# Attention jobs of the two layers: heads paired across the key groups, values of four jobs as one product

## The reference

```python
q = partial_rope(rmsnorm_2(q, q_norm[l]), cos, sin)          # 16 heads
k = partial_rope(rmsnorm_2(k, k_norm[l]), cos, sin)          # 2 heads
a_out = sliding_window_attention(q, k, v, sinks[l])
c_out = conformer_conv(u, ug, conv_w[l], conv_b[l], conv_ln_g[l],
                       conv_ln_b[l], w_conv_out[l])
merged = jax.nn.sigmoid(ga) * a_out + jax.nn.sigmoid(gb) * c_out
x = x + jnp.einsum('btd,de->bte', merged, w_out[l])
```

## Time and profile before

| | |
|---|---|
| median of 3 runs | 2248.43 us (2248.36 to 2249.26) |
| span of the profiled execution | 2246.4 us |
| TensorE busy | 2224.9 us, 99% |
| VectorE busy | 1245.1 us, 55% |
| ScalarE busy | 885.6 us, 39% |
| GpSimd busy | 280.7 us, 12% |
| granted TensorE clock | 0.999 of full |
| stage of the job loop | 1033 to 1155 us and, the second time, 1725 to 1847 us |

### The profile page before, as it was taken

The page is one execution under the profiler, slowest core; times in us unless marked ns, Lnnn a source line. Parts: engine busy times, 40 slices in busy tenths (PEclk is TensorE's granted clock), DMA queues, the critical chain, the costliest instruction groups (busy, mean ns, idle before and its releaser), DMA issues.

```text
span 2246.4 us, 29245 instructions
## 1 busy us (share of the span) xinstructions
PE 2224.9 (99%) x11388; PEld 1821.7 (81%) x11388; DVE 1245.1 (55%) x1836; ACT 885.6 (39%) x1363; POOL 280.7 (12%) x273
## 2 busy tenths in 40 slices
PE   9999999999999999999999999999999999999999
PEld 7877888898888888886778888888887668888887
DVE  6467656445444225999664444333889664544422
ACT  5545454354333225234744333222323753433321
POOL 3000032011000001014331000001003442000000
PEclk9999999999999999999999999999999999999999
DMA  6221033122222231321122222222221112322222
GB/s 223 100 76 57 20 121 126 55 72 99 103 102 93 94 113 69 113 75 57 56 77 81 107 93 93 100 106 105 104 84 57 39 66 85 113 102 104 94 101 86
DMA packets 30484, 203.19 MB, mean 90 GB/s; under 512 B 3504, under 2 KB 4144, under 8 KB 6704
## 3 DMA queue, kind: packets, MB, share of 16 engines
q1 hardware_dynamic: 29088, 197.34, 24.4%
q10 hardware_dynamic: 1296, 4.46, 0.5%
HBM read 199.69 MB, written 2.10 MB: 90 GB/s over the span
## 4 chain that ended last, share of the span: by engine, by line
PE 93%; DVE 3%; POOL 1%; ACT 1%; issue 1%; DMA 0%; ACTq 0%; DVEq 0%; POOLq 0%
PE bank L415 26%; PE bank L417 26%; PE bank L416 26%; PE bank L2110 1%; PE bank L1002 1%; PE bank L2120 1%; PE bank L2133 1%; PE bank L973 1%; PE bank L2028 1%; POOL acc L324 1%; PE bank L990 1%; PE bank L2010 1%; PE bank L1593 1%; PE bank L1570 1%; PE bank L515 1%
## 5 line engine op out<-in xcount | busy, mean ns | idle before, releaser
L415 PE MATMUL bank<-x_hi,w_hi 128*128 128x512 f32 (+1 forms) x2032 | 789.9, 389 | 5.9 <-DVE x_lo L1766 2.3
L417 PE MATMUL bank<-x_hi,w_lo 128*128 128x512 f32 (+1 forms) x2032 | 775.0, 381 | 0.0
L416 PE MATMUL bank<-x_lo,w_hi 128*128 128x512 f32 (+1 forms) x2032 | 774.1, 381 | 0.0
L301 DVE TENSOR_TENSOR w_lo<-w_raw,w_hi 128x2048 fp32r<-128x2048 f32 x167 | 386.2, 2313 | 412.3 <-ACT w_hi L297 412.3
L297 ACT ACTIVATE w_hi<-w_raw 128x2048 fp32r<-128x2048 f32 x167 | 319.7, 1916 | 585.8 <-PE bank L417 583.9
L415 PEld LDWEIGHTS bank<-x_hi,w_hi 128*128 128x128 f32 x2032 | 382.1, 188 | 83.6 <-issue 6.8
L417 PEld LDWEIGHTS bank<-x_hi,w_lo 128*128 128x128 f32 x2032 | 381.9, 188 | 74.9
L416 PEld LDWEIGHTS bank<-x_lo,w_hi 128*128 128x128 f32 x2032 | 382.4, 188 | 72.7 <-issue 2.9
L415 PE MATMUL bank<-f_hi,w_hi 128*128 128x512 f32 (+1 forms) x572 | 213.3, 373 | 0.0
L416 PE MATMUL bank<-f_lo,w_hi 128*128 128x512 f32 (+1 forms) x572 | 213.2, 373 | 0.0
L417 PE MATMUL bank<-f_hi,w_lo 128*128 128x512 f32 (+1 forms) x572 | 213.2, 373 | 0.0
(11 more groups left out here) (355 smaller groups left out, 2637.2 us busy)
## 6 DMA issues: line engine op xcount, KB each, us to landing
w_raw<-w_d SPq DMA_DIRECT2D x184, 1024.0 KB, 4.8
out_d<-h SPq DMA_DIRECT2D x8, 256.0 KB, 6.6
h<-x_d ACTq DMA_DIRECT2D x3, 512.0 KB, 9.2
tab<-rope_d ACTq DMA_DIRECT2D x2, 640.0 KB, 3.9
memT<-mem_d ACTq DMA_DIRECT2D x1, 1024.0 KB, 4.8
w_raw<-w_d SPq DMA_DIRECT2D x2, 256.0 KB, 4.1
h<-x_d ACTq DMA_DIRECT2D x2, 256.0 KB, 5.8
w_raw<-w_d SPq DMA_DIRECT2D x1, 512.0 KB, 6.6
```

The source lines that it names most:

```text
L301: dve.tensor_tensor(w_lo[:, u.slot, :], w_raw[:, u.slot, :], w_hi[:, u.slot, :], ALU.subtract).then_inc(lo_ready, 1)
L415: pe.matmul(dst, wh[:, k, cols], hi[:, kx_, at:at + width], start=start, stop=False)
L416: pe.matmul(dst, wh[:, k, cols], lo[:, kx_, at:at + width], start=False, stop=False)
L417: return pe.matmul(dst, wl[:, k, cols], hi[:, kx_, at:at + width], start=False, stop=stop)
```

## The change

- Query heads are stored so that tile t holds head t on the lower and head 8 + t on the upper half of the partitions. Both halves then find their keys in place: lkx and its two ScalarE copies a layer go. The host orders the columns of the query, attention gate and convolution gate weights, of the convolution's output weights, the rows of the output weights and the sinks to match.
- The value product takes a group of four jobs (two in block 0): lprobT holds four jobs side by side, one matmul moves up to 512 columns. There are ten groups, in steps 7, 11, 15, 19, 23, 27, 29, 31, 33 and 35, and each stands between the scores and the transposes of its step. The gating is one VectorE instruction a group.
- FILL_AT deals the same 75 chunks out otherwise: fewer in the steps with values, more in others.
- VectorE merges tiles 3, 5 and 7, GpSimd 0, 1, 2, 4 and 6. MERGE_HI_AT goes from 29 to 31, MERGE_LO_AT from 30 to 32, and OUT_AT from one tile in each of steps 32 to 35 to tile 0 in step 32, tile 1 in 34, tiles 2 and 3 in 35.

```diff
@@ scratch @@
-        lkx = place("lkx", [P, T], F32, a)
-        lprobT = place("lprobT", [P, 2, 4, P], F32, b)
+        lprobT = place("lprobT", [P, 2, 2, 4, P], F32, b)
@@ groups and schedule @@
+        GROUPS = [range(j, j + 4) for j in range(0, 24, 4)] + [range(j, j + 2) for j in range(24, LJ, 2)]
+        NG = len(GROUPS)
+        GROUP_OF = [n for n, js in enumerate(GROUPS) for _ in js]
+        VALUES_AT = {js[-1] + LAG_V: n for n, js in enumerate(GROUPS)}
-        FILL_AT = {1: 6, 2: 2, 3: 1, 5: 4, 6: 4, 7: 2, 9: 3, 10: 2, 12: 3, 14: 6, 15: 5, 16: 3, 17: 4, 18: 4, 19: 2,
-                   20: 3, 21: 2, 22: 1, 23: 2, 24: 2, 25: 2, 26: 1, 27: 2, 28: 2, 29: 3, 30: 3, 31: 1}
+        FILL_AT = {1: 6, 2: 3, 4: 1, 5: 4, 6: 4, 7: 1, 8: 3, 9: 3, 10: 2, 12: 3, 13: 2, 14: 3, 15: 1, 16: 4, 17: 3, 18: 3,
+                   19: 1, 20: 4, 21: 3, 22: 3, 23: 1, 24: 3, 25: 3, 26: 2, 27: 1, 28: 3, 29: 1, 30: 3, 31: 1}
-        MERGE_HI_AT, MERGE_LO_AT = 29, 30
-        OUT_AT = {32: (0,), 33: (1,), 34: (2,), 35: (3,)}
+        MERGE_HI_AT, MERGE_LO_AT = 31, 32
+        MERGED_BY_DVE, MERGED_BY_POOL = (3, 5, 7), (0, 1, 2, 4, 6)
+        OUT_AT = {32: (0,), 34: (1,), 35: (2, 3)}
@@ TensorE @@
-                    keys = key_rows(lq[:, 8, :], lkx[:, :], e, g)[:, k0:(i + 1) * P]
+                    keys = lq[HD * e:HD * e + HD, 8, k0:(i + 1) * P]
-            def values(j):
+            def values(n):
+                js, cols = GROUPS[n], group_cols(n)
-                pe.wait_ge(A["turned_copied"], L * LJ + j + 1)
+                pe.wait_ge(A["turned_copied"], L * LJ + js[-1] + 1)
...
-                        mm = pe.matmul(bank[HD * e:HD * e + HD, 6, 0:P], lv[:, i - 1 + c, g * HD:(g + 1) * HD],
-                                       lprobT[:, j % 2, 2 * e + c, :], start=(c == first), stop=(c == 1))
+                        mm = pe.matmul(bank[HD * e:HD * e + HD, 6, cols.start * P:cols.stop * P], lv[:, i - 1 + c, e * HD:(e + 1) * HD],
+                                       lprobT[:, e, c, cols, :].rearrange("p m t -> p (m t)"), start=(c == first), stop=(c == 1))
@@ order of a step @@
+                if t in VALUES_AT:
+                    values(VALUES_AT[t])
                 if 0 <= t - LAG_T < LJ:
                     turn(t - LAG_T)
                 fill_chunks(FILL_AT.get(t, 0))
...
-                if 0 <= t - LAG_V < LJ:
-                    values(t - LAG_V)
@@ ScalarE @@
-                if n == ROPE_UNITS[0] + 2:
-                    act.wait_ge(q_rope, L * 9 + 1)
-                    act.activation(lkx[0:HD, :], lq[HD:P, 8, :], ACT.Copy).then_inc(l_kx, 1)
-                    act.activation(lkx[HD:P, :], lq[0:HD, 8, :], ACT.Copy).then_inc(l_kx, 1)
-                if j >= 2:
-                    act.wait_ge(A["pv"], L * LJ + j - 1)
+                if j >= 4:
+                    act.wait_ge(A["pv"], L * NG + GROUP_OF[j - 4] + 1)
@@ VectorE @@
-                if 0 <= t - LAG_V < LJ:
-                    gated(t - LAG_V)
-                if t == STEPS - 1:
-                    dve.wait_ge(A["gated"], L * LJ + LJ)
-                    dve.wait_ge(mg_sum, L * 8 + 7)
-                    dve.wait_ge(co_ready, L * 8 + 8)
-                    dve.tensor_tensor(sgb[:, 7, :], sgb[:, 7, :], sga[:, 7, :], ALU.add).then_inc(mg_sum, 1)
+                if t in VALUES_AT:
+                    gated(VALUES_AT[t])
+                if t in (LJ - 1, LJ + 1, LJ + 3):
+                    k = MERGED_BY_DVE[(t - LJ + 1) // 2]
+                    dve.wait_ge(A["gated"], L * NG + GROUP_OF[24 + k] + 1)
+                    dve.wait_ge(co_ready, L * 8 + k + 1)
+                    dve.tensor_tensor(sgb[:, k, :], sgb[:, k, :], sga[:, k, :], ALU.add).then_inc(mg_sum_dve, 1)
@@ GpSimd @@
-                    if j > 28:
-                        merged(L, j - 29)
-                for k in range(LJ - 28, DT - 1):
+                    if j in (LJ - 2, LJ - 1):
+                        merged(L, j - LJ + 2)
+                for k in MERGED_BY_POOL[2:]:
                     merged(L, k)
```

More of the change, by code:

```diff
@@ L2098, in scores @@
             def scores(j):
[L2099 removed]
+                i, tile = block_of(j), j % 8
                 if j == 0:
[L2101 removed]
                     pe.wait_ge(l_g, L * 16 + 10)
@@ L2419, in softmax, with gated @@
                     dve.reciprocal(asm(o, 12), asm(o, 4)).then_inc(A["rec"], 1)
[L2421 to L2425 removed]
+            def gated(n):
+                js, cols = GROUPS[n], group_cols(n)
+                i, tile = block_of(js[0]), js[0] % 8
+                dst = sga[:, tile:tile + len(js), i * P:(i + 1) * P]
+                dve.wait_ge(A["pv"], L * NG + n + 1)
+                if n == 0:
                     dve.wait_ge(l_g, L * 16 + 8)
[L2427 removed]
+                pv = bank[:, 6, cols.start * P:cols.stop * P].rearrange("p (m t) -> p m t", t=P)
+                dve.scalar_tensor_tensor(out=dst, in0=dst, scalar=1.0, in1=pv, op0=ALU.add, op1=ALU.mult).then_inc(A["gated"], 1)
             def conv_gated(k):
@@ L2699 @@
     stream += ffn_units(g["w_gate_up"], g["w_down"])
+    paired = np.concatenate([np.r_[HD * t:HD * t + HD, HD * (8 + t):HD * (8 + t) + HD] for t in range(8)])
+    sink_order = np.arange(16).reshape(2, 8).T.reshape(-1)
     for l in range(LAYERS):
```

47 lines of the change are left out of this document (26 added, 21 removed).

## The result

The changed kernel is slower: 2258.94 us (2257.43 to 2260.06) against 2248.68 (2248.36 to 2249.26) for the kernel before, ratio 1.0044 with a 95% interval of 1.0032 to 1.0056, so 10.3 us. The forecast was 2252.2 us, with a range up to 2256.5: the direction held, the size did not.

What follows compares the result with a forecast made beforehand. TensorE, busy 99% of the span, was taken as the bound. Per layer, 0.75 us gained before the last fill less 2.6 lost at the end, doubled, made a 3.7 us loss on 2248.43: 2252.2 us, range 2242.5 to 2256.5.

Steps and rivals of the forecast that it cites:

- Part 1: Value products in TensorE's queue: four jobs as one product take 1.87 us instead of 2.36, saving 3.0 us a layer.
- F: End of the last fill product in a layer's attention stage, 1141.94 us in the kernel before.
- Part 2: Dropping the swapped keys and their two ScalarE copies a layer: 0, bound a gain of 0.7 us a layer.
- Part 3: New order before the last block: new TensorE waits cost 0.3, 0.15 and 1.8 us a layer.
- the column sums: At step 7 TensorE comes earlier and waits longer for GpSimd: cost 0.3 us a layer.
- step 12: Its transposes wait for ScalarE's copy because step 11 has no fill: cost 0.15 us a layer.
- ScalarE's chain: Steps 14 to 17: step 17's transposes wait for ScalarE's chain, cost 1.8 us a layer, bounds 0 and 2.1.
- The net before F: Balance before the last fill: 3.0 - 0.3 - 0.15 - 1.8, about +0.75 us gained a layer.
- Rivals 1 and 4: Waits stay small, 2244.5 us, chance 0.20; or TensorE's savings and waits cancel, 2248.4 us, chance 0.20.
- rival 3: The 512-column value pairs do not overlap: 10 us a layer more, about 2270 us; chance 0.02.
- part 4: End of the stage, last fill to output product k=4: loss of 0.8 to 4.4 us a layer, 2.6 taken.
- rival 2: The tail's far end: VectorE loses the port at k=0, k=1 and k=3, 2255.7 us; chance 0.18.

Runs made afterwards that it cites:

- e2: Kernel before with paired heads, no swapped keys and groups of four in the first 24 jobs, old fill and old end: 2245.85 us against 2248.11.
- e1: Kernel before with only paired heads and no swapped keys, groups of one, old fill, merges and output products: 2248.44 us against 2248.11.
- e4: Changed kernel with ten spare TensorE products before output product k=0 and six before k=1: 2253.55 us against 2248.11 for the kernel before.
- e8: Changed kernel with tile 7 alone merged by VectorE, tiles 0 to 6 by GpSimd: 2252.87 us against 2249.13 for the kernel before.
- e9: Changed kernel, GpSimd's first merges a step earlier, halves from steps 30 and 31, o_lo before gating, VectorE merging only tile 7: 2247.59 us against 2248.96 before.
- e12: e9 with two fill chunks moved from step 17 to step 16: 2245.64 us against 2248.96 for the kernel before.
- e10: e2 with the new fill up to step 12, then the old less a chunk in steps 14, 19 and 23: 2244.70 us against 2248.96 before.
- e11: e10 with high and low halves of the output tiles one step later, from steps 30 and 31: 2261.16 us against 2248.96 for the kernel before.

## Why the prediction was wrong

**Right.** The bound, and that the waits of TensorE decide. Part 1: 1.87 a group was predicted and 1.86 measured; 3.0 us a layer predicted and 2.6 measured, in e2 and in the changed kernel alike (there 0.6 net plus 2.0 of new waits before F: 0.81 + 0.17 + 0.57 + 0.15 + 1.49 = 3.2 against 1.2); the rest is short waits that the list leaves out. Part 2 at nothing: e1. Part 3: the column sums 0.3 predicted and 0.57 - 0.26 = 0.31 measured; step 12 0.15 predicted and 0.85 - 0.63 = 0.22 measured (1074.34 to 1075.19); ScalarE's chain 1.8 predicted and 0.15 + 1.49 = 1.64 measured (TensorE's side of that sum is 3.3 + 3.8 + 4.0 + 0.6 = 11.7, not 11.6, so it gives 1.7). The net before F was predicted at +0.75 a layer and is +0.6. Rivals 1 and 4 fell with the waits at the end, and rival 3 with the 1.86.

**The step that failed is part 4,** the end of the stage, taken as 2.6 us a layer and measured as 6.9 and 5.4. Two errors are in it.

The first is a term that was mis-sized. I worked the end out between 13.7 and 17.3 us behind F, and took the middle, "since rows 9 show the port lost once and elsewhere it isn't". Without the half clock the end is 19.8 - 3.0 = 16.8 and 18.4 - 1.6 = 16.8, and e4 measures the same: a loss of 3.9 a layer, nearer the far end than the 2.6. The port was lost at k=0 and at k=1, and k=3 was 0.69 late, as rival 2 had it. Worse, the reason beside it, that moving merges between the two engines would not alter who holds the port, was wrong: in e8, with two of them moved back, VectorE's o_lo holds it at k=1, and the end takes 1.3 us a layer less at full clock (6.5 us in the medians, with the half clock that doesn't follow). I had priced a merge by its duration on the port and not by what it does to the order. It stood between a gating and an o_lo, and let GpSimd start first.

The second is a term that was missing: the half clock. Every product in the sum was priced at full clock, also behind waits that I had forecast myself at 2 us and more. It cost 3.0 and 1.6 us in the profiled execution, 4.8 in the medians (e4). With 3.9 instead of 2.6 and this term the forecast's own sum gives (0.75 - 3.9) x 2 = -6.3, and -4.8 more: 2248.4 + 11.1 = 2259.5, against 2258.9 measured. Rival 2, the far end of the forecast at 2255.7, was priced at full clock too; the mis-sized term alone would have stayed inside the range (2254.7), and it is the missing one that left it.

What the expected gain turned into: the groups of four took 2.6 x 2 = 5.2 us off TensorE before F, and 4.0 of them came back there as waits for ScalarE's and GpSimd's chains. The end then took 12.3. With the end put in order (e9) and the fill too (e12) the change's own groups are 3.3 us faster than the kernel before, and e10, with groups of four and the old end, 4.3; the stages of the traces say 2.8 and 2.6.

## What to carry to other kernels

An engine's queue order is a price of its own: before a step is moved behind one that waits for another engine, ask whether that engine waits for the moved step. A ring of two engines costs its full length every turn, and one step of lead hides it (e11: 16.5 us for one constant, 10.9 of them the ring and its waits). And where a forecast contains new waits of TensorE, price what follows at both clock levels: in the stages the clock fell behind waits of 2.48, 1.98 and 1.72, and behind 1.52 and 1.58 with one of 0.56 shortly before, but not every time. Last, compare a stage in two traces before comparing two medians: here the first block alone moved a time by up to 4 us.
